# Where the operands of a matmul lie in SBUF: start addresses on multiples of 64 bytes, with a gap between held and streamed operands

## The chip, the cores and the metric

The kernel runs on one core of one Trainium2 chip. The metric is the device time of one execution in microseconds. The kernel before took 2775.96 us (median of 3 runs, 2774.65 to 2776.91). The profile is of one execution of its own.

## The reference: what is computed

One layer of an encoder over 2048 tokens of width 1024, all in float32:

```
h    = rms_norm(x) * g
proj = h @ w_in                       # 1024 -> 7 groups of 512 columns
A    = differential attention over 4 heads (block-causal mask, two softmax maps per head)
B    = HGRN2 gated linear recurrence over 4 heads, chunks of 64 tokens
x    = x + concat(A, B) @ w_out       # 1024 -> 1024
x    = x + (silu(h2 @ w_gate) * (h2 @ w_up)) @ w_down   # h2 = rms_norm(x) * g2, 1024 -> 2816 -> 1024
```

## The kernel before

All large products are made of the same piece, a matmul on TensorE of 128 rows by 128 columns held in the array against 512 columns streamed through it, in the type float32r. To keep float32 accuracy, each operand is split into a high part (a copy rounded to float32r, by ScalarE) and a low part (the remainder, by VectorE), and each product is a triple of matmuls: high by high, high by low, low by high. In a statement `pe.matmul(dst, held, streamed, ...)` the second argument is the held operand (128 columns, 512 bytes in a partition) and the third is the streamed one (512 columns, 2048 bytes in a partition). In the rows of the profile the order is the other way round: `out<-streamed,held`.

Each matmul is preceded by a weight load (LDWEIGHTS, the row PEld), which reads the held operand of the next matmul while the present one is streaming. So at nearly all times TensorE reads SBUF in two places: the streamed operand of one matmul and the held operand of another.

The kernel has four stages, one after the other:

- `project` (names `proj_`): h @ w_in in 4 blocks of 512 tokens. h of a block is in `h_hi[b % 2]` and `h_lo[b % 2]`. `h_hi[0]` is no tensor of its own: it is the tensor `lend_lent`, lent from outside. `h_hi[1]` is `proj_h_hi1`. Blocks 0 and 2 use `lend_lent`, blocks 1 and 3 use `proj_h_hi1`; nothing else differs between them. The weights are in `proj_w_hi`, `proj_w_lo`. For five of the seven groups of columns the weights are streamed and h is held (L667 to L669), for two it is the reverse (L663 to L665).
- `mix_tokens` (`att_`, `rec_`): attention and recurrence, with many small matmuls (128 or 64 columns) and some of 512 columns (`att_ring`, L1221 and L1224: keys streamed, queries held).
- `feed` (`feed_`): x + mix @ w_out, and the gate and up products, by Strassen's scheme of seven products. The held operands are `feed_a_hi`, `feed_a_lo`, the streamed ones `feed_b_hi` and `feed_b_lo`, seven of each; of the seven low parts two lie in `lend_lent` (L1867 to L1869). These go to the banks x and y, for half of the matmuls of L1868 each that the bank receives.
- `down` (`down_`): the last product, in the same scheme. Held: `down_f_hi`, `down_f_lo`; streamed: `down_w_hi`, `down_w_lo` (L2142 to L2144).

The order of the work is written out by hand in one block per engine, with semaphores between them; no scheduler or pool decides anything. Only the helper `Alloc.sb` (L75) says where a tensor lies: it takes the next free place in SBUF, so addresses follow from the order of the calls and from the sizes. A tensor starts on a multiple of 32 bytes; so a tensor of 4 bytes in a partition takes 32, and all that comes after it is displaced by 32.

Of the kernel before, what the change touches and what calls it, by code (L numbers as in the profile page):

```python
# [8 lines left out]

# [1 line left out]

# [3 lines left out]
P = 128  # L17
# [32 lines left out]
F32 = mybir.dt.float32  # L50
# [18 lines left out]
class Alloc:  # L69
# [3 lines left out]
        self.nc, self.ctx, self.prefix = nc, ctx, prefix  # L73

    def sb(self, name, shape, dt=F32):  # L75
        return self.ctx.enter_context(self.nc.sbuf_tensor(f"{self.prefix}_{name}", shape, dt))

    def bank(self, name):
        return self.ctx.enter_context(self.nc.psum_tensor(f"{self.prefix}_{name}", [P, 512], F32))
# [107 lines left out]
def project(nc, x, attn_g, w_in, q_g, k_g, ident, pair_sel, eps, out, masks, early, lambdas, subln_g, hgrn_g, w_out,  # L187
# [19 lines left out]
    with ExitStack() as ctx:  # L207
        a = Alloc(nc, ctx, "proj")
# [8 lines left out]
        warm = a.sb("warm", [P, 1])  # L217
        h_hi = [early.lent[:].rearrange("p a (s n) -> p (a s) n", n=TB), a.sb("h_hi1", [P, KS, TB], F32R)]
        h_lo = [a.sb(f"h_lo{b}", [P, KS, TB], F32R) for b in range(2)]
        w_raw = [a.sb(f"w_raw{b}", [P, KH, W]) for b in range(2)]  # L220
        w_hi = [a.sb(f"w_hi{b}", [P, KH, W], F32R) for b in range(2)]
        w_lo = [a.sb(f"w_lo{b}", [P, KH, W], F32R) for b in range(2)]
# [1119 lines left out]
def feed(nc, x, mix, ffn_g, w_gate, w_up, ident, eps, x_mid, out_operands, operands, ff, first_full, first_full_in,  # L1342
# [19 lines left out]
    with ExitStack() as ctx:  # L1362
        a = Alloc(nc, ctx, "feed")
        g_col = a.sb("g_col", [P, KS])
        full = [first_full, a.sb("full", [P, OPERANDS + 1, HALF_SLABS, P])[:]]
        a_hi = a.sb("a_hi", [P, OPERANDS, HALF_SLABS, P], F32R)
        a_lo = a.sb("a_lo", [P, OPERANDS, HALF_SLABS, P], F32R)
        b_hi = [a.sb(f"b_hi{i}", [P, HALF_SLABS * TB], F32R) for i in range(OPERANDS)]
        b_lo = [*first_b, *(a.sb(f"b_lo{i}", [P, HALF_SLABS * TB], F32R)[:] for i in range(len(first_b), OPERANDS))]
        results = [a.sb(f"results{k}", [P, 4, TB]) for k in range(2)]  # L1370
# [505 lines left out]
def down(nc, ff, w_down, x_mid, y, stored):  # L1876
# [19 lines left out]
    with ExitStack() as ctx:  # L1896
        a = Alloc(nc, ctx, "down")
        w_raw = [a.sb(f"w_raw{b}", [P, 2, D]) for b in range(RAWS)]
        w_hi = [a.sb(f"w_hi{b}", [P, SLABS, COLS], F32R) for b in range(2)]
        w_lo = [a.sb(f"w_lo{b}", [P, SLABS, COLS], F32R) for b in range(2)]  # L1900
        f_raw = [a.sb(f"f_raw{b}", [P, SLABS, P]) for b in range(2)]
        f_hi = [a.sb(f"f_hi{b}", [P, SLABS, P], F32R) for b in range(2)]
        f_lo = [a.sb(f"f_lo{b}", [P, SLABS, P], F32R) for b in range(2)]
# [244 lines left out]
def hybrid_trunk_kernel(nc, x, attn_norm_g, w_in, q_norm_g, k_norm_g, lambda_q1, lambda_k1, lambda_q2, lambda_k2,  # L2148
# [16 lines left out]
    with ExitStack() as ctx:  # L2165
        a = Alloc(nc, ctx, "all")
        ident, ones = (a.sb(n, [P, P]) for n in ("ident", "ones"))
        pair_sel = a.sb("pair_sel", [P, 2])
        eps = a.sb("eps", [P, 1])
        y_stored = [a.sem(f"y_stored{b}") for b in range(4)]  # L2170
        early_in = [a.sem(f"early_{n}_in") for n in ("k", "q", "rf", "rqk", "small")]
        first_full_in, *first_b_in = (a.sem(f"first_{n}_in") for n in ("full", "b0", "b1"))
        make_constants(nc, ident, pair_sel, ones, eps)
        with ExitStack() as whole:
            lending = Alloc(nc, whole, "lend")
            shared = lending.sb("shared", [P, 2, HEADS * TB])
            lent = lending.sb("lent", [P, 2, HALF_SLABS * TB], F32R)
            first_full = shared[:].rearrange("p a (b s n) -> p (a b) s n", s=HALF_SLABS, n=P)
            first_b = [lent[:, i, :] for i in range(2)]
            with ExitStack() as both:  # L2180
                early = First(Alloc(nc, both, "early"), early_in, shared, lent)
                masks = Alloc(nc, both, "level").sb("masks", [P, HGRN_LEVELS, HEADS // 2 * TB // 2], mybir.dt.uint8)
                last_spent = project(nc, x[0], attn_norm_g[0], w_in[0], q_norm_g[0], k_norm_g[0], ident, pair_sel, eps, mid, masks,
                                     early, (lambda_q1[0], lambda_k1[0], lambda_q2[0], lambda_k2[0]), subln_g[0], hgrn_norm_g[0],
                                     w_out[0], out_operands)

                nc.gpsimd.sem_clear(range(first_b_in[-1].num + 1, last_spent + 1))
                mix_tokens(nc, mid, ident, eps, masks, mix, early, out_operands, first_full, first_full_in, first_b, first_b_in)
            feed(nc, x[0], mix, ffn_norm_g[0], w_gate[0], w_up[0], ident, eps, x_mid, out_operands, operands, ff, first_full,
                 first_full_in, first_b, first_b_in)  # L2190
        down(nc, ff, w_down[0], x_mid, out[0], y_stored)
# [27 lines left out]
```

## Time and profile before

| | us |
|---|---|
| median of 3 runs | 2775.96 |
| the profiled execution, whole | 2776.23 |
| its span, first to last instruction | 2774.5 |
| TensorE (PE) busy | 2634.8 (95%) |
| weight loads (PEld) busy | 2214.1 (80%) |
| VectorE (DVE) busy | 1557.5 (56%) |
| ScalarE (ACT) busy | 1131.1 (41%) |
| GpSimd (POOL) busy | 896.2 (32%) |
| mean granted TensorE clock | 0.982 of full speed |

How to read it: matmuls overlap each other in the profile, since each is drawn with its way through the array (0.39 us for 512 columns), while the next one starts 0.23 us after it. So the busy time tells that TensorE always has work, but not how fast it goes. The rate is read from the distance between the starts of successive matmuls in the rows in order of time. A busy 95% together with a start every 0.23 us means that the time of the kernel is the number of matmuls by that distance, and a few waits.

The 512-column matmuls of `proj_`, `feed_` and `down_` make up some 2033 us of the 2774.5: 8904 of them at 0.2267 to 0.2332 us each.

### The profile page before, as it was taken

The page shows a single profiled execution, that of the slowest core. Times are in us where ns is not written, and L with a number is a line of the kernel's source. Part 1 is how long each engine was busy: PE and PEld are TensorE (multiplying, and loading weights), DVE is VectorE, ACT ScalarE, POOL GpSimd, SP SyncE. Part 2 cuts the span into 40 slices and gives each one's busy share as a digit, 9 for nine tenths or more (in the row PEclk, how much of TensorE's full clock was granted, in tenths as well). Part 3 has the DMA queues.
Part 4 walks back from the last instruction along what each step waited for, and adds up shares of the span by engine and source line. Part 5 has one row for each costly group of instructions (what it writes and reads, how often), then busy time and mean ns, then how long its engine had stood idle before and what let it go on. Part 6 is the DMA issues. An engine that isn't in the chain of part 4 may idle for free. (4 is left out here: it accounts for less than half of the span.)

```text
span 2774.5 us, 34306 instructions
## 1 busy us (share of the span) xinstructions
PE 2634.8 (95%) x13288; PEld 2214.1 (80%) x13288; DVE 1557.5 (56%) x1906; ACT 1131.1 (41%) x1922; POOL 896.2 (32%) x607
## 2 busy tenths in 40 slices
PE   7999999999999999986998999998999997999999
PEld 6888888887888888875776888886888885888887
DVE  5434344333676767656677565657666664356653
ACT  4434344332567666674444222224222222332231
POOL 5001100002424242303556454555454451135400
PEclk9999999999999999997998999999999998999999
DMA  4755555384343433315675334345333333777763
GB/s 154 257 181 198 172 192 198 121 282 130 100 112 102 112 101 84 92 35 197 227 254 187 98 101 111 99 114 178 110 103 104 95 102 119 260 274 266 250 208 127
DMA packets 343874, 430.48 MB, mean 155 GB/s; under 512 B 19232, under 2 KB 212768, under 8 KB 341024
## 3 DMA queue, kind: packets, MB, share of 16 engines
q1 hardware_dynamic: 343712, 428.29, 49.2%
q8 instruction: 106, 1.74, 0.3%
q14 instruction: 56, 0.46, 0.1%
HBM read 301.87 MB, written 129.50 MB: 155 GB/s over the span
## 5 line engine op out<-in xcount | busy, mean ns | idle before, releaser
L522 DVE TENSOR_TENSOR proj_w_lo<-proj_w_raw,proj_w_hi 128x2048 fp32r<-128x2048 f32 x56 | 129.8, 2318 | 233.6 <-ACT proj_w_hi L422 233.6
L2142 PE MATMUL down_prod<-down_w_hi,down_f_hi 128*128 128x512 f32 x616 | 241.2, 391 | 19.8 <-DVE down_f_lo L2078 18.9
L669 PE MATMUL proj_prod<-proj_w_hi,proj_h_lo 128*128 128x512 f32 x640 | 251.5, 393 | 0.0
L2143 PE MATMUL down_prod<-down_w_lo,down_f_hi 128*128 128x512 f32 x616 | 240.3, 390 | 0.0
L2144 PE MATMUL down_prod<-down_w_hi,down_f_lo 128*128 128x512 f32 x616 | 240.1, 390 | 0.0
L1621 ACT ACTIVATE feed_a_hi<-lend_shared 128x1024 fp32r<-128x1024 f32 (+1 forms) x78 | 94.1, 1207 | 325.7 <-PE feed_v_bank L1869 162.5
L1015 ACT ACTIVATE att_expo<-att_ring,att_neg_max 128x1024 f32<-128x1024 f32 (+4 forms) x192 | 164.8, 862 | 92.7 <-DVE att_neg_max L1126 74.0
L2048 ACT ACTIVATE down_f_hi<-down_f_raw 128x768 fp32r<-128x768 f32 x112 | 83.0, 786 | 281.8 <-PE down_prod L2144 279.0
L1621 ACT ACTIVATE feed_a_hi<-feed_full 128x1024 fp32r<-128x1024 f32 (+1 forms) x78 | 94.0, 1205 | 236.8 <-PE feed_y_bank L1869 155.2
L1867 PE MATMUL feed_y_bank<-feed_b_hi,feed_a_hi 128*128 128x512 f32 x416 | 165.7, 398 | 17.8 <-DVE feed_results L1748 17.8
L1867 PE MATMUL feed_x_bank<-feed_b_hi,feed_a_hi 128*128 128x512 f32 x416 | 163.2, 392 | 12.7 <-DVE lend_lent L1717 12.7
L1712 DVE TENSOR_TENSOR feed_a_lo<-lend_shared,feed_a_hi 128x1024 fp32r<-128x1024 f32 (+1 forms) x78 | 131.2, 1682 | 66.1 <-ACT feed_a_hi L1621 66.0
L1867 PE MATMUL feed_v_bank<-feed_b_hi,feed_a_hi 128*128 128x512 f32 x416 | 163.5, 393 | 3.4 <-DVE feed_results L1766 3.4
L1712 DVE TENSOR_TENSOR feed_a_lo<-feed_full,feed_a_hi 128x1024 fp32r<-128x1024 f32 (+1 forms) x78 | 143.3, 1837 | 40.1 <-ACT feed_a_hi L1621 40.1
L1869 PE MATMUL feed_y_bank<-feed_b_hi,feed_a_lo 128*128 128x512 f32 x416 | 164.9, 396 | 0.0
L1869 PE MATMUL feed_x_bank<-feed_b_hi,feed_a_lo 128*128 128x512 f32 x416 | 163.9, 394 | 0.0
L1868 PE MATMUL feed_v_bank<-feed_b_lo,feed_a_hi 128*128 128x512 f32 x416 | 162.6, 391 | 0.0
L1869 PE MATMUL feed_v_bank<-feed_b_hi,feed_a_lo 128*128 128x512 f32 x416 | 162.4, 390 | 0.0
L1121 DVE TENSOR_REDUCE att_run_neg_max<-att_ring 128x1 f32<-128x1024 f32 (+7 forms) x128 | 120.7, 985 | 60.6 <-PE att_ring L1224 60.6
L2142 PEld LDWEIGHTS down_prod<-down_w_hi,down_f_hi 128*128 128x128 f32 x616 | 116.0, 188 | 46.6 <-DVE down_f_lo L2078 19.8
L422 ACT ACTIVATE proj_w_hi<-proj_w_raw 128x2048 fp32r<-128x2048 f32 x56 | 107.2, 1914 | 105.8 <-PE proj_prod L669 75.2
L669 PEld LDWEIGHTS proj_prod<-proj_w_hi,proj_h_lo 128*128 128x128 f32 x640 | 120.5, 188 | 28.1
(254 smaller groups left out, 6860.4 us busy)
## 6 DMA issues: line engine op xcount, KB each, us to landing
proj_w_raw<-in_w_in_dram SPq DMA_DIRECT2D x56, 1024.0 KB, 6.5
lend_shared<-in_w_gate_dram SPq DMA_DIRECT2D x88, 256.0 KB, 4.1
feed_full<-in_w_up_dram SPq DMA_DIRECT2D x88, 256.0 KB, 4.1
ff<-feed_results SPq DMA_DIRECT2D x88, 256.0 KB, 2.6
down_w_raw<-in_w_down_dram SPq DMA_DIRECT2D x22, 1024.0 KB, 7.9
down_f_raw<-ff SPq DMA_DIRECT2D x56, 384.0 KB, 3.3
down_f_raw<-ff SPq DMA_DIRECT2D x56, 320.0 KB, 3.6
ff<-feed_ff_sum SPq DMA_DIRECT2D x66, 256.0 KB, 3.2
```

The source lines that it names most:

```text
L522: nc.vector.tensor_tensor(w_lo[n % 2][:], w_raw[n % 2][:], w_hi[n % 2][:].bitcast(F32), ALU.subtract).then_inc(w_lo_made, 1)
L669: last = pe.matmul(prod[t][:], lo[:, s, tile], wh[:, k, :], start=False, stop=stop)
L1015: nc.scalar.activation(expo[b][:, m, key:key + width], ring[:, bank * 512:bank * 512 + width], ACT.Exp, bias=neg_max[:, b, m:m + 1], accum ...
L1121: last = nc.vector.tensor_reduce(dst, ring[:, bank * 512:bank * 512 + width], AX.X, ALU.max, negate=True)
L1621: nc.scalar.activation(a_hi[:, first:end], full[g % 2][:, first:end], ACT.Copy).then_inc(a_hi_made, 1)
L1712: nc.vector.tensor_tensor(a_lo[:, first:end], full[g % 2][:, first:end], a_hi[:, first:end].bitcast(F32), ALU.subtract).then_inc(a_lo_made, 1)
L1867: pe.matmul(dst, a_hi[:, pos, s, :], hi, start=opens and s == 0, stop=False, skip_group_check=True)
L1868: pe.matmul(dst, a_hi[:, pos, s, :], lo, start=False, stop=False, skip_group_check=True)
L1869: last = pe.matmul(dst, a_lo[:, pos, s, :], hi, start=False, stop=s == HALF_SLABS - 1, skip_group_check=True)
L2142: pe.matmul(dst, hi[:, s, :], wh[:, s, :], start=opens and s == 0, stop=False, skip_group_check=True)
L2143: pe.matmul(dst, hi[:, s, :], wl[:, s, :], start=False, stop=False, skip_group_check=True)
L2144: last = pe.matmul(dst, lo[:, s, :], wh[:, s, :], start=False, stop=closes and s == SLABS - 1, skip_group_check=True)
```

## The change

The change touches addresses alone. No instruction is added, removed or reordered; the number of rows of the program is the same on each engine, and only line numbers differ (by 1 to 13).

- `Alloc.sb` rounds each tensor up to a multiple of 64 bytes: if its size in units of 32 bytes is odd, it is followed by an unused tensor of 32 bytes.
- In `project`, 128 unused bytes stand between `h_lo` and the weights; in `feed`, 128 between `a_lo` and `b_hi`; in `down`, 64 between `w_lo` and `f_raw`.

```diff
     def sb(self, name, shape, dt=F32):
-        return self.ctx.enter_context(self.nc.sbuf_tensor(f"{self.prefix}_{name}", shape, dt))
+
+        tensor = self.ctx.enter_context(self.nc.sbuf_tensor(f"{self.prefix}_{name}", shape, dt))
+        size = math.prod(shape[1:]) * (1 if dt == mybir.dt.uint8 else 4)
+        if -(-size // 32) % 2:
+            self.gap(name, 32)
+        return tensor
+
+    def gap(self, name, size):
+
+        self.ctx.enter_context(self.nc.sbuf_tensor(f"{self.prefix}_{name}_gap", [P, size // 4], F32))
...
         h_lo = [a.sb(f"h_lo{b}", [P, KS, TB], F32R) for b in range(2)]
+        a.gap("h_lo", 128)
         w_raw = [a.sb(f"w_raw{b}", [P, KH, W]) for b in range(2)]
...
         a_lo = a.sb("a_lo", [P, OPERANDS, HALF_SLABS, P], F32R)
+        a.gap("a_lo", 128)
         b_hi = [a.sb(f"b_hi{i}", [P, HALF_SLABS * TB], F32R) for i in range(OPERANDS)]
...
         w_lo = [a.sb(f"w_lo{b}", [P, SLABS, COLS], F32R) for b in range(2)]
+        a.gap("w_lo", 64)
         f_raw = [a.sb(f"f_raw{b}", [P, SLABS, P]) for b in range(2)]
```

What it does to the places that TensorE reads. Every held piece and every streamed piece begins a multiple of 512 bytes after the start of its tensor, so what two operands have to do with each other is told by their start addresses modulo 512 (bytes within a partition, from the compiled programs):

| operand | before | after |
|---|---|---|
| `lend_lent` | 192 | 256 |
| `proj_h_hi1`, `proj_h_lo` | 480 | 320 |
| `proj_w_hi`, `proj_w_lo` | 480 | 448 |
| `att_k_rest`, `att_q` (own tensors) | 256 | 384 |
| `early_k` | 192 | 256 |
| `feed_a_hi`, `feed_a_lo` | 224 | 320 |
| `feed_b_hi`, `feed_b_lo` (own tensors) | 224 | 448 |
| `down_w_hi`, `down_w_lo` | 192 | 256 |
| `down_f_hi`, `down_f_lo` | 192 | 320 |

Held less streamed, modulo 512:

| pair | before | after |
|---|---|---|
| project, h own, weights streamed | 0 | 384 |
| project, h in `lend_lent`, weights streamed | 224 | 320 |
| project, h own streamed, weights held | 0 | 128 |
| project, `lend_lent` streamed, weights held | 288 | 192 |
| feed, own tensors | 0 | 384 |
| feed, `lend_lent` streamed, a held | 32 | 64 |
| down | 0 | 64 |

Before, the distance of every pair with `lend_lent` is an odd multiple of 32, and of every other pair of the three large stages it is 0. After, every distance is a multiple of 64 and none is 0.

## Rows read from the trace of the kernel before

**Rows 1.** The page: its span, and TensorE in part 1.
```profile
span 2774.5 us, 34306 instructions
PE 2634.8 (95%) x13288; PEld 2214.1 (80%) x13288; DVE 1557.5 (56%) x1906; ACT 1131.1 (41%) x1922; POOL 896.2 (32%) x607
```

**Rows 2.** Groups of instructions by line, project: busy us, mean ns | idle before.
```profile
L667 PE MATMUL proj_prod<-proj_w_hi,lend_lent 128*128 128x512 f32 x320 | 129.9, 406 | 6.8 <-DVE proj_w_lo L522 6.0 <-DVE proj_h_lo L536 0.7
L668 PE MATMUL proj_prod<-proj_w_lo,lend_lent 128*128 128x512 f32 x320 | 127.7, 399 | 0.0
L667 PE MATMUL proj_prod<-proj_w_hi,proj_h_hi 128*128 128x512 f32 x320 | 125.7, 393 | 0.0
L668 PE MATMUL proj_prod<-proj_w_lo,proj_h_hi 128*128 128x512 f32 x320 | 124.6, 389 | 0.0
...
L663 PE MATMUL proj_prod<-lend_lent,proj_w_hi 128*128 128x512 f32 x128 | 51.1, 399 | 0.0
L663 PE MATMUL proj_prod<-proj_h_hi,proj_w_hi 128*128 128x512 f32 x128 | 50.2, 392 | 0.0
```

**Rows 3.** The same view, feed and down.
```profile
L2142 PE MATMUL down_prod<-down_w_hi,down_f_hi 128*128 128x512 f32 x616 | 241.2, 391 | 19.8 <-DVE down_f_lo L2078 18.9 <-DVE down_w_lo L2072 0.8
...
L1867 PE MATMUL feed_y_bank<-feed_b_hi,feed_a_hi 128*128 128x512 f32 x416 | 165.7, 398 | 17.8 <-DVE feed_results L1748 17.8
...
L1867 PE MATMUL feed_v_bank<-feed_b_hi,feed_a_hi 128*128 128x512 f32 x416 | 163.5, 393 | 3.4 <-DVE feed_results L1766 3.4
L1867 PE MATMUL feed_x_bank<-feed_b_hi,feed_a_hi 128*128 128x512 f32 x416 | 163.2, 392 | 12.7 <-DVE lend_lent L1717 12.7
...
L1868 PE MATMUL feed_x_bank<-lend_lent,feed_a_hi 128*128 128x512 f32 x208 | 83.5, 401 | 0.0
...
L1868 PE MATMUL feed_y_bank<-lend_lent,feed_a_hi 128*128 128x512 f32 x208 | 82.6, 397 | 0.0
L1867 PE MATMUL feed_z_bank<-feed_b_hi,feed_a_hi 128*128 128x512 f32 x208 | 81.0, 390 | 0.4 <-DVE feed_b_lo L1717 0.4
...
L1868 PE MATMUL feed_x_bank<-feed_b_lo,feed_a_hi 128*128 128x512 f32 x208 | 80.9, 389 | 0.0
```

**Rows 4.** TensorE in time, project, block 0: start us, us, what; 89 rows, ends.
```profile
99.38 0.39 PE L664 MATMUL proj_prod<-proj_h_lo,proj_w_hi 128*128 128x512 f32 x1
...
119.90 0.39 PE L669 MATMUL proj_prod<-proj_w_hi,proj_h_lo 128*128 128x512 f32 x1
```

**Rows 5.** The same, block 1 (`proj_h_hi1`): 112 rows, ends.
```profile
249.78 0.39 PE L664 MATMUL proj_prod<-proj_h_lo,proj_w_hi 128*128 128x512 f32 x1
...
274.94 0.39 PE L664 MATMUL proj_prod<-proj_h_lo,proj_w_hi 128*128 128x512 f32 x1
```

**Rows 6.** The same, feed with `lend_lent`: 15 rows, ends.
```profile
2139.45 0.40 PE L1869 MATMUL feed_x_bank<-feed_b_hi,feed_a_lo 128*128 128x512 f32 x1
...
2142.68 0.40 PE L1868 MATMUL feed_y_bank<-lend_lent,feed_a_hi 128*128 128x512 f32 x1
```

**Rows 7.** The same, down: 134 rows, ends.
```profile
2449.71 0.39 PE L2143 MATMUL down_prod<-down_w_lo,down_f_hi 128*128 128x512 f32 x1
...
2479.85 0.39 PE L2144 MATMUL down_prod<-down_w_hi,down_f_lo 128*128 128x512 f32 x1
```

**Rows 8.** The same, feed, first matmuls of 512 columns after transposes.
```profile
1308.22 0.40 PE L1868 MATMUL feed_y_bank<-feed_b_lo,feed_a_hi 128*128 128x512 f32 x1
...
1308.69 0.39 PE L1867 MATMUL feed_y_bank<-feed_b_hi,feed_a_hi 128*128 128x512 f32 x1
1308.91 0.39 PE L1868 MATMUL feed_y_bank<-feed_b_lo,feed_a_hi 128*128 128x512 f32 x1
...
1309.84 0.39 PE L1869 MATMUL feed_y_bank<-feed_b_hi,feed_a_lo 128*128 128x512 f32 x1
```

**Rows 9.** Who waited for whom: us in total, times, longest.
```profile
ACT down_f_hi L2048 <- PE down_prod L2144: 279.0, 53, 6.0
ACT feed_a_hi L1621 <- PE feed_y_bank L1869: 272.9, 80, 11.5
...
DVE proj_w_lo L522 <- ACT proj_w_hi L422: 233.6, 56, 12.4
```

More of the change, by code:

```diff
@@ L12 @@
+import math
 from contextlib import ExitStack
```

## The prediction

> **What bounds the kernel now.** I read first the span and busy times of the page: TensorE is busy for 2634.8 of 2774.5 us, no other engine for more than 56% [rows 1]. Then the groups by line: the triples of 512-column matmuls of project, feed and down carry the time, and the idle time ahead of them is small, 6.8 us at the most in project, 17.8 and 12.7 in feed, 19.8 in down [rows 2, 3]. Then the waits: the longest ones are of ScalarE for TensorE, 279.0 us in down and 272.9 in feed; VectorE waits 233.6 us for ScalarE in project, with TensorE going on [rows 9]. So TensorE is the bound in these stages, and a matmul that costs less there shortens the kernel.
>
> The view that decides is the last, TensorE's rows in order of time, since the distance between starts is what a matmul costs. In a stretch of project with h in `lend_lent`, 89 rows in a row without a gap go from 99.38 to 119.90 us: 20.52 / 88 = 0.2332 us each [rows 4]. In a stretch of the block with `proj_h_hi1`, 112 rows take 25.16 us: / 111 = 0.2267 [rows 5]. In feed, where one of three streamed operands is `lend_lent`, 15 rows take 3.23 us: / 14 = 0.2307, which is one hundredth of a microsecond in 3.23 uncertain [rows 6]. In down, 134 rows take 30.14 us: / 133 = 0.2266 [rows 7]. At the 2.4 GHz that the granted clock of 1.0 in these stretches stands for, streaming 512 columns takes 213.3 ns, so even the best stretch has 13 ns a matmul too much.
>
> The same instructions on the same weights, in blocks that differ only in where h lies, are 6.5 ns apart. The groups by line say it too: L667 has a mean of 406 ns with `lend_lent` and 393 without, L668 399 and 389, L663 399 and 392; in feed L1868 has 401 with `lend_lent` and 389 without [rows 2, 3]. Since TensorE reads the next held operand while it streams, I take it that the two reads get into each other's way, and that their distance modulo some small power of two sets how much: 0 costs 13 ns, an odd multiple of 32 costs 20.
>
> One more thing is in the rows. After transposes, the first 512-column matmuls of feed with distance 0 are not at 0.2267: from 1308.22 to 1309.84 us seven steps take 1.62, that is 0.2314, and the steps vary, one of them being 0.22 [rows 8]. Only later do they settle. So the cost depends on how the two reads meet in time as well, and 0.2267 is a state into which the sequence falls, not a constant of the address.
>
> **The change, part by part.** It is addresses only, so the sum is a count of matmuls by a difference of steps.
>
> *Multiples of 64.* All distances that were odd multiples of 32 are now even ones. In project with `lend_lent` there are 320 triples with h held and 128 with h streamed [rows 2]: 448 x 3 = 1344 matmuls. If they go from 0.2332 to 0.2267, that is 1344 x 6.5 ns = 8.7 us. In feed `lend_lent` is in 208 + 208 = 416 triples [rows 3], 1248 matmuls, which go from 0.2307 to 0.2267: 5.0 us. Together 13.7 us. The two ends: 0, if what matters is a coarser distance than 64 (then 64 is as bad as 32), and 13.7 us. What speaks for the upper end is that the stages at distance 0 hold 0.2267 with held pieces at any multiple of 512. I take 13.7.
>
> *Gaps of 128 and 64.* All 8904 matmuls (448 + 448 triples in project; 1456 in feed, from 416 + 416 + 416 + 208 of L1867; 616 in down; 2968 x 3) [rows 2, 3] now have a distance that is not 0. The trace has no long stretch at such a distance, so this is the unknown term. One end: the reads no longer meet, and a step is 213.3 ns; the other: the settled state of distance 0 is lost, and each step costs the unsettled mean, 231.4 ns [rows 8]. Against 226.7, these are -13.4 and +4.7 ns a matmul, -119 us over all 8904 and, for the 6312 without `lend_lent` alone, +30 us. The nearest row to a better state is the shortest step of rows 8, 1308.69 to 1308.91, shown as 0.22; as its neighbours average 0.231 I read it as 0.224 (an estimate from the rounded starts; it could be up to 0.225 and some less). It shows that one meeting of the reads at 2.7 ns less is possible; that a whole sequence holds it isn't shown. I take half of that way, 1.3 ns: 8904 x 1.3 = 11.6 us.
>
> *Everything else.* The attention stage has some 500 matmuls of 512 columns, in groups of 2 to 7 that never settle; at 5 ns either way this is under 3 us, put at 0. The 32-byte shifts of the operands of ScalarE, VectorE, GpSimd and of the DMAs are put at nothing: these engines wait for TensorE by the hundreds of microseconds [rows 9], and a few per cent of their operations stay under that cover. Should TensorE become so fast that the cover goes, the first to be late is VectorE in feed, the one whose results it waits for even now (17.8 us) [rows 3].
>
> Sum for the profiled execution, 2776.2 us whole (span 2774.5 and 1.7 around it; the median of the runs is 2776.0, so nothing has to be shifted): 2776.2 - 13.7 - 11.6 = 2750.9, say 2750.
>
> **The rule that speaks against it.** The rows show 0.2332 beside 0.2267 us for the same lines with another place of h [rows 4, 5]. The Trainium skill, "TensorE: Matmul & The Clock Gate", section "Step-by-step: what each phase is for", says that TensorE has two independent SBUF read ports and that loading the next weights takes nothing from the running matmul; "SBUF — State Buffer", section "Who interferes with whom", says that TensorE never waits for anyone there. By that rule no address would matter and the time would stay at 2776. By this trace it doesn't hold in full.
>
> **The rivals.**
>
> *Alignment helps, the gaps do nothing.* A sequence at any constant distance that is a multiple of 64 settles into the same state, since the two reads shift in time against each other until they fit. For it: the settling in rows 8, and that down and own-tensor project have the same 0.2267 [rows 5, 7]. Time: 2776.2 - 13.7 = 2762.5.
>
> *No change at all.* Either what slows the `lend_lent` blocks isn't the 32 bytes but the mixture of distances in a triple (in project 224, 224, 0), which goes on after the change (320, 320, 384), and a constant distance costs the same everywhere; or reads do not interfere and the difference has another source in that tensor. For it: in the mixed triples the matmul with own-tensor operands, L669 or L1869, is slow as well, as the even 0.2332 over all rows shows [rows 4]. Time: 2776.
>
> *Slower: the settled state is lost.* At a distance of 0 modulo 512 the sequence holds 0.2267. If this state exists only there, the change takes it away in down (64), feed (384) and project (384, 128), and all 6312 matmuls outside `lend_lent` go at 0.2314: 6312 x 4.7 ns = 30 us; `lend_lent` stays where it is. Time: 2806. It decides even against a full gain of the alignment if more than about 2900 matmuls (13.7 us / 4.7 ns) lose the state; feed with own tensors, 3120 of them, is enough. For it: it is the only state seen to hold in 25 to 30 us without a break [rows 5, 7]; against it: that an unsettled sequence at all distances would have to find no state of its own.
>
> *Conflicts gone.* 213.3 ns a step: 8904 steps make 1899 us in place of 1344 x 0.2332 + 1248 x 0.2307 + 6312 x 0.2267 = 2032. Time: 2776 - 133 = 2643. Against it: no step in the rows is under 0.22.
>
> **How the numbers follow.** The forecast (both help, the gaps by a little) 0.42, its own range 2735 to 2762; alignment alone 0.20 (2762.5); no change 0.12 (2776); slower 0.18 (2806, or less where only one stage loses its state); conflicts gone 0.08 (2643). Faster by over 0.2% (5.5 us, about what a measurement of this kernel can tell from no change) is 0.42 + 0.20 + 0.08 = 0.70, the same 0.12, slower 0.18. The range of 8 in 10 takes in the forecast, alignment alone, no change, and the third of the slower case in which one stage alone loses its state: 2700 to 2795. Below, it reaches to gaps that are worth some 7 ns a matmul.
>
> **What would show it.** In the changed kernel, TensorE's rows in time: project with `lend_lent` at 0.2267 or under (alignment right), at 0.233 (wrong); down at 0.224 to 0.226 (gap right), at 0.2267 (gaps do nothing), at 0.231 and never settling (slower rival), at 0.215 (conflicts gone). Down has no `lend_lent` and was at distance 0, so it tells the gap alone; project before and after tells both. The groups by line should show L667 with `lend_lent` and with `proj_h_hi` at the same mean. ScalarE's waits for TensorE should shrink by what TensorE gains. The prediction is wrong if the gain is in the attention stage or in waits rather than in the steps, or if down moves opposite to project.

## The result and the profile after

The changed kernel takes 2809.2 us (median of 4 runs, 2808.45 to 2811.59) beside 2776.4 us of the kernel before on the same chips: 1.0119 times, 95% interval 1.0106 to 1.0133. It is slower by some 33 us; 2750 was forecast, with 2700 to 2795 as the range.

The page, in the rows that answer to [rows 1], shows the same instructions, with TensorE busy 36 us longer:

```profile
span 2807.6 us, 34306 instructions
...
PE 2671.0 (95%) x13288; PEld 2220.0 (79%) x13288; DVE 1550.5 (55%) x1906; ACT 1129.8 (40%) x1922; POOL 896.2 (32%) x607
```

By stage (TensorE alone; columns: stretch in us from the span's start, its length, PE busy with the count of matmuls, granted clock, share of the DMA engines, GB/s), first the kernel before, cut at the ends of project, mix_tokens and feed:

```profile
0.00:669.00 669.00, 650.99 (x2942) 1.00 0.56 188
669.00:1262.00 593.00, 536.82 (x4004) 0.97 0.37 100
1262.00:2340.00 1078.00, 1024.66 (x4496) 0.98 0.44 135
2340.00:2775.00 435.00, 422.29 (x1848) 0.99 0.70 232
```

and the changed one:

```profile
0.00:675.00 675.00, 656.93 (x2944) 1.00 0.55 186
675.00:1268.00 593.00, 537.48 (x4000) 0.96 0.36 100
1268.00:2361.00 1093.00, 1042.02 (x4496) 0.98 0.43 133
2361.00:2808.00 447.00, 434.59 (x1848) 0.98 0.68 226
```

Project is 6 us longer, feed 15, down 12, the attention stage as before. TensorE's busy time grows by 5.9, 17.4 and 12.3 us; in feed some of it goes into waits that it had anyway. The granted clock is the same (0.981 over the span, 0.982 before), so it isn't the clock.

TensorE's rows in order of time (start us, us, what), first down, which answers to [rows 7], 131 rows without a gap:

```profile
2479.65 0.39 PE L2156 MATMUL down_prod<-down_w_lo,down_f_hi 128*128 128x512 f32 x1
...
2509.99 0.39 PE L2157 MATMUL down_prod<-down_w_hi,down_f_lo 128*128 128x512 f32 x1
```

30.34 / 130 = 0.2334 us a matmul, where it was 0.2266. Project with `proj_h_hi1`, which answers to [rows 5], 109 rows:

```profile
249.64 0.39 PE L675 MATMUL proj_prod<-proj_h_lo,proj_w_hi 128*128 128x512 f32 x1
...
274.84 0.39 PE L675 MATMUL proj_prod<-proj_h_lo,proj_w_hi 128*128 128x512 f32 x1
```

25.20 / 108 = 0.2333 for 0.2267. Project with `lend_lent`, which answers to [rows 4], 88 rows:

```profile
99.79 0.40 PE L674 MATMUL proj_prod<-lend_lent,proj_w_hi 128*128 128x512 f32 x1
...
119.99 0.40 PE L678 MATMUL proj_prod<-proj_w_hi,lend_lent 128*128 128x512 f32 x1
```

20.20 / 87 = 0.2322 for 0.2332: here the change gains a little. The groups by line, which answer to [rows 2, 3] (busy us, mean ns | idle before), say the same, and also that the waits ahead of the largest groups are about what they were (19.5 us for 19.8 in down, 17.7 for 17.8 in feed):

```profile
L2155 PE MATMUL down_prod<-down_w_hi,down_f_hi 128*128 128x512 f32 x616 | 245.1, 398 | 19.5 <-DVE down_f_lo L2091 19.3 <-DVE down_w_lo L2085 0.2
...
L1879 PE MATMUL feed_y_bank<-feed_b_hi,feed_a_hi 128*128 128x512 f32 x416 | 166.3, 400 | 17.7 <-DVE feed_results L1760 17.7
...
L678 PE MATMUL proj_prod<-proj_w_hi,proj_h_hi 128*128 128x512 f32 x320 | 127.3, 398 | 0.0
...
L679 PE MATMUL proj_prod<-proj_w_lo,proj_h_hi 128*128 128x512 f32 x320 | 126.3, 395 | 0.0
L679 PE MATMUL proj_prod<-proj_w_lo,lend_lent 128*128 128x512 f32 x320 | 125.8, 393 | 0.0
...
L1880 PE MATMUL feed_x_bank<-lend_lent,feed_a_hi 128*128 128x512 f32 x208 | 83.1, 399 | 0.0
```

L679 (L668 before) has 395 ns with `proj_h_hi` for 389, and 393 with `lend_lent` for 399: the two have changed places. ScalarE's waits for TensorE, which answer to [rows 9], grow with TensorE's steps:

```profile
ACT feed_a_hi L1633 <- PE feed_y_bank L1881: 295.6, 84, 11.3
ACT down_f_hi L2061 <- PE down_prod L2157: 291.2, 53, 6.2
```

The sum of the steps nearly closes. Over all starts that are under 300 ns apart in both traces, the mean step changes like this:

| matmuls of 512 columns | number | before, ns | after, ns | together, us |
|---|---|---|---|---|
| down | 1848 | 226.7 | 233.3 | +12.1 |
| feed without `lend_lent` | 3120 | 226.9 | 232.4 | +16.9 |
| feed with `lend_lent` | 1248 | 231.1 | 231.6 | +0.6 |
| project, own h held | 960 | 227.2 | 232.8 | +5.3 |
| project, own h streamed | 384 | 227.0 | 233.1 | +2.3 |
| project, `lend_lent` held | 960 | 233.1 | 231.2 | -1.8 |
| project, `lend_lent` streamed | 384 | 233.0 | 232.0 | -0.4 |

Together that is 35 us, beside 36.2 more of busy time and 33.1 more of span; TensorE's idle time is 3.1 us less (136.6 for 139.7).

### The profile page after: what moved, and what is told of

Same layout as the page of the kernel before. It is cut to its first block and busy times, and to the rows that moved or that the text cites. A ratio compares the mean times of both kernels' runs of the same rounds, so it can differ in the third digit from the quotient of the medians.

```text
span 2807.6 us, 34306 instructions
## 1 busy us (share of the span) xinstructions
PE 2671.0 (95%) x13288; PEld 2220.0 (79%) x13288; DVE 1550.5 (55%) x1906; ACT 1129.8 (40%) x1922; POOL 896.2 (32%) x607
## 5 line engine op out<-in xcount | busy, mean ns | idle before, releaser
L2155 PE MATMUL down_prod<-down_w_hi,down_f_hi 128*128 128x512 f32 x616 | 245.1, 398 | 19.5 <-DVE down_f_lo L2091 19.3
L1879 PE MATMUL feed_y_bank<-feed_b_hi,feed_a_hi 128*128 128x512 f32 x416 | 166.3, 400 | 17.7 <-DVE feed_results L1760 17.7
L1724 DVE TENSOR_TENSOR feed_a_lo<-feed_full,feed_a_hi 128x1024 fp32r<-128x1024 f32 (+1 forms) x78 | 139.7, 1791 | 40.2 <-ACT feed_a_hi L1633 40.2
```

The source lines that it names most:

```text
L1724: nc.vector.tensor_tensor(a_lo[:, first:end], full[g % 2][:, first:end], a_hi[:, first:end].bitcast(F32), ALU.subtract).then_inc(a_lo_made, 1)
L1879: pe.matmul(dst, a_hi[:, pos, s, :], hi, start=opens and s == 0, stop=False, skip_group_check=True)
L2155: pe.matmul(dst, hi[:, s, :], wh[:, s, :], start=opens and s == 0, stop=False, skip_group_check=True)
```

## The experiments

Ahead of the runs stood the theory that the slower rival had put: at a distance of 0 (held less streamed, by start addresses) the sequence of matmuls settles at 226.7 ns, and the gaps took that away. "Distance" is modulo 512 bytes below, until the runs reduce it. The two operands that meet are the one being streamed and the one being loaded beside it for the next matmul.

**The rounding alone.** The changed kernel without its gaps:

```diff
         h_lo = [a.sb(f"h_lo{b}", [P, KS, TB], F32R) for b in range(2)]
-        a.gap("h_lo", 128)
...
-        a.gap("a_lo", 128)
...
-        a.gap("w_lo", 64)
```

> The rounding to 64 bytes alone, without the three gaps. Own-tensor operands are at distance 0 modulo 512 again, lend_lent 64 from the rest. Theory 1 (the gaps took the settled state of distance 0 away): down and the triples without lend_lent are back at 226.7 ns a matmul, those with lend_lent stay at 231 to 233; time 2770 to 2778 us. Rival (the rounding, by what it does to absolute addresses, is what slows): down stays at 233 ns, time 2800 to 2812 us. Second rival (64 bytes from the rest is as good as 0 for a triple with lend_lent): those at 226.7 too, time about 2762 us.

Measured: 2772.3 us, 0.9986 times the kernel before (0.9976 to 0.9995). Down is at 226.7 ns again, and so are the settled stretches of project and feed without `lend_lent`. In down 135 rows take 30.38 us, / 134 = 0.2267:

```profile
2449.62 0.39 PE L2154 MATMUL down_prod<-down_w_hi,down_f_lo 128*128 128x512 f32 x1
...
2480.00 0.39 PE L2153 MATMUL down_prod<-down_w_lo,down_f_hi 128*128 128x512 f32 x1
```

The triples with `lend_lent`, 64 bytes from the rest, have 229.2 ns in project with h held and 229.4 in feed, less than at odd multiples of 32 (233.1 and 231.1), but not 226.7. In project with h streamed they have 234.0, where they had 233.0: this got worse, and it is outside the 231 to 233 that were expected. So the first theory holds for the operands that are back at distance 0, and the rounding is worth some 4 us by itself, where 13.7 was forecast.

**The gaps alone**, the other half: the kernel before with the three gaps and no rounding.

```diff
         h_lo = [a.sb(f"h_lo{b}", [P, KS, TB], F32R) for b in range(2)]
+        a.gap("h_lo", 128)
...
         a_lo = a.sb("a_lo", [P, OPERANDS, HALF_SLABS, P], F32R)
+        a.gap("a_lo", 128)
...
         w_lo = [a.sb(f"w_lo{b}", [P, SLABS, COLS], F32R) for b in range(2)]
+        a.gap("w_lo", 64)
```

> The three gaps alone, without the rounding to 64 bytes. Distances of own-tensor operands are 64 (down), 384 (feed) and 384, 128 (project), as in the changed kernel; those with lend_lent are odd multiples of 32. Theory (what the change costs is the loss of the settled state at distance 0, and the rounding only moves lend_lent by a little): down at 233.3, own-tensor triples of feed and project at 232 to 233, lend_lent at 231 to 234; time 2776 + 6312 x 6 ns = 2814 us, less 2 for the beginnings, 2808 to 2816 us. Rival (the two parts cost only together): 2776 to 2790 us.

Measured: 2808.2 us, 1.0116 times (1.0099 to 1.0132), as the whole change. In down 130 rows take 30.11 us, / 129 = 0.2334:

```profile
2479.78 0.40 PE L2150 MATMUL down_prod<-down_w_hi,down_f_hi 128*128 128x512 f32 x1
...
2509.89 0.39 PE L2150 MATMUL down_prod<-down_w_hi,down_f_hi 128*128 128x512 f32 x1
```

The gaps carry the whole loss. The two parts do not add up: the 4 us of the rounding are not there when the gaps are (2808.2 us without it, 2809.2 with it).

**Everything at distance 0.** The kernel before, with two pieces of padding that bring h, the weights and feed's operands to the residue of `lend_lent`, 192:

```diff
+        a.gap("h_hi", 224)
         h_hi = [early.lent[:].rearrange("p a (s n) -> p (a s) n", n=TB), a.sb("h_hi1", [P, KS, TB], F32R)]
...
         g_col = a.sb("g_col", [P, KS])
+        a.gap("g_col", 480)
         full = [first_full, a.sb("full", [P, OPERANDS + 1, HALF_SLABS, P])[:]]
```

> The kernel before with 224 unused bytes ahead of proj_h_hi1 and 480 behind feed's g_col, so that every held and streamed operand of project and feed, lend_lent among them, is at distance 0 modulo 512. Theory 1 (distance 0 is what lets the steps settle at 226.7 ns): all triples of project and feed at 226.7, time 2776.4 - 1344 x 6.5 ns - 1248 x 4.4 ns = 2762 us. Rival (lend_lent is slow for another reason than its distance): its triples stay at 233 and 231 ns, time 2776 us.

Measured: 2764.0 us, 0.9952 times (0.9940 to 0.9965), 12 us less than before by the medians (2775.9) and 13 by the ratio. The theory's number was 2762. All settled steps are at 226.7 ns, those with `lend_lent` too, and the groups show it: L673, L674 and L1875 here are L667, L668 and L1868 of [rows 2, 3].

```profile
L673 PE MATMUL proj_prod<-proj_w_hi,lend_lent 128*128 128x512 f32 x320 | 127.8, 399 | 6.8 <-DVE proj_w_lo L528 6.0 <-DVE proj_h_lo L542 0.8
L673 PE MATMUL proj_prod<-proj_w_hi,proj_h_hi 128*128 128x512 f32 x320 | 125.6, 393 | 0.0
L674 PE MATMUL proj_prod<-proj_w_lo,lend_lent 128*128 128x512 f32 x320 | 125.4, 392 | 0.0
...
L1875 PE MATMUL feed_x_bank<-lend_lent,feed_a_hi 128*128 128x512 f32 x208 | 81.9, 394 | 0.0
L1875 PE MATMUL feed_y_bank<-lend_lent,feed_a_hi 128*128 128x512 f32 x208 | 80.9, 389 | 0.0
```

About half of what is left between 399 and 393 ns in L673 is in the first twelve matmuls of block 0, from 20.9 to 25.7 us, four of which are of L673: the granted clock is 0.50 there, TensorE's lower level of 1.2 GHz, after a stretch in which it was nearly idle (3.7 us busy of 20), and most of the twelve have 0.63 us in place of 0.39. In the starts, which the comparison rests on, nothing is left: the steps from the tenth on behind a break have 226.7 ns in both blocks. So `lend_lent` was slow for its distance.

**The attention stage as well.** The same with `a.gap("first", 448)` ahead of att's tensors.

> As e2_zero, and 448 unused bytes ahead of att's tensors, so that keys and queries of the attention stage, too, are at distance 0 from one another and from lend_lent. Theory: its some 500 matmuls of 512 columns stand in groups of 2 to 7, too short to settle, so the gain over e2_zero is 0 to 2 us: 2761 to 2764 us. Rival (a mixture of distances costs 6 ns a matmul there too): 500 x 6 ns = 3 us, and the groups of att_ring have a mean that is 6 ns less.

Measured: 2764.5 us, 0.9955 times (0.9942 to 0.9967), no different from the run before it. Where two 512-column matmuls of `att_ring` follow each other within 250 ns (185 times), the mean step is 231.5 ns here and 231.3 without that padding: they come in groups of one to seven, shorter than the nine steps that settling takes elsewhere (below).

**Which distances settle.** Two sweeps give each of the two buffers of an operand a place of its own, so that one run holds four distances in down and four more in project. In down, where w0, w1 are the streamed and f0, f1 the held buffers, the first sweep has this (the second puts 256 bytes more ahead of f0):

```diff
-        w_hi = [a.sb(f"w_hi{b}", [P, SLABS, COLS], F32R) for b in range(2)]
-        w_lo = [a.sb(f"w_lo{b}", [P, SLABS, COLS], F32R) for b in range(2)]
+        w_hi, w_lo = [], []
+        for k, part in enumerate((w_hi, w_lo)):
+            part.append(a.sb(f"w_part{k}0", [P, SLABS, COLS], F32R))
+            a.gap(f"w_up{k}", 448)
+            part.append(a.sb(f"w_part{k}1", [P, SLABS, COLS], F32R))
+            a.gap(f"w_down{k}", 64)
...
+        for k, part in enumerate((f_hi, f_lo)):
+            part.append(a.sb(f"f_part{k}0", [P, SLABS, P], F32R))
+            a.gap(f"f_up{k}", 128)
...
```

> Distances (held less streamed, modulo 512) by buffer: in down 0, 64 for f_hi0 and 128, 192 for f_hi1, by w_hi0 and w_hi1; in project 32, 160 (blocks 0 and 2) and 224, 352 (blocks 1 and 3), with the negatives where h is streamed; feed all 0. Theory 1: 226.7 ns in down's 0 and in feed, 230 to 234 at every other distance. Rival (each distance has a settled state of its own level): levels that differ, some perhaps under 226.7. Second rival (only whether a distance is constant counts, so that distance 64 costs the same as 0 in long stretches): all of down at one level.

> As the sweep before it, with 256, 320 (f_hi0) and 384, 448 (f_hi1) in down, and 96, 128 and 352, 384 in project. Theory 1 in its form with a period of 512 bytes: none at 226.7, all at 230 to 234 ns. If the period is 256 bytes: the distance 256 is at 226.7. If it is 128: 256 and 384 are.

Measured (2785.2 and 2789.0 us, single runs): one stretch of down in the first sweep passes from distance 0 to 128 at 2604.54 us, when `f_hi1` is held in place of `f_hi0`, the streamed buffer being the same:

```profile
2599.78 0.39 PE L2170 MATMUL down_prod<-down_w_part,down_f_part 128*128 128x512 f32 x1
...
2604.54 0.40 PE L2170 MATMUL down_prod<-down_w_part,down_f_part 128*128 128x512 f32 x1
...
2611.99 0.39 PE L2169 MATMUL down_prod<-down_w_part,down_f_part 128*128 128x512 f32 x1
```

21 steps of 0.2267 us (4.76 us) and then 32 of 0.2328 (7.45 us). The means by distance, worked out from all starts of the two traces, from the tenth step in a row at one distance on:

| held less streamed, modulo 512 | mean step, ns | where |
|---|---|---|
| 0 | 226.7 | down, feed |
| 256 | 226.7 | down |
| 32 | 233.5 | project |
| 64, 320 | 233.3, 233.3 | down |
| 96 | 234.0 | project |
| 128, 384 | 232.3, 232.4 | down |
| 128, 384 | 232.6, 232.7 | project |
| 160, 416 | 233.3, 233.3 | project |
| 192, 448 | 231.1, 231.1 | down |
| 224, 480 | 233.3, 233.4 | project |
| 352 | 234.3 | project |

Two distances that are 256 apart have the same value within 0.3 ns: the period is 256 bytes, so my modulus of 512 was twice too large, and of the multiples of 32 only 0 has the low level. The best of the others is 192. The 64 and 128 of the changed kernel are among the others. Away from 0 the distance isn't all: at 128, with h streamed, the same lines of project have 233.3 ns in the changed kernel and 232.5 with the gaps alone, and what differs there is only where the whole lies.

**The same gaps at 256.** If so, the changed kernel needs no more than another number:

```diff
-        a.gap("h_lo", 128)
+        a.gap("h_lo", 256)
...
-        a.gap("a_lo", 128)
+        a.gap("a_lo", 256)
...
-        a.gap("w_lo", 64)
+        a.gap("w_lo", 256)
```

> The changed kernel with its three gaps at 256 bytes in place of 128, 128 and 64, nothing else. Theory (the settled state at 226.7 ns comes back every 256 bytes of distance, and the gaps of 128 and 64 took it away): down, and the triples of project and feed without lend_lent, at 226.7 ns; those with lend_lent, 64 from the rest, at 229 to 231 as with the rounding alone; time 2768 to 2775 us. Rival (any gap, or what it displaces behind it, slows): 2795 to 2812 us, down at 231 to 234 ns.

Measured: 2773.2 us, 0.9985 times (0.9976 to 0.9995), as with the rounding alone. In down 134 rows take 30.15 us, / 133 = 0.2267:

```profile
2449.74 0.39 PE L2155 MATMUL down_prod<-down_w_hi,down_f_hi 128*128 128x512 f32 x1
...
2479.89 0.39 PE L2156 MATMUL down_prod<-down_w_lo,down_f_hi 128*128 128x512 f32 x1
```

The settled steps of feed (226.8) and of project (226.7) at distance 256 say the same. The triples with `lend_lent` are again at 229.1 and 229.4, and at 234.0 with h streamed, over the 231 that was expected. A gap does no harm by itself; its size modulo 256 does.

**Small distances.** In down each tensor is 256 bytes longer and its operand begins a few bytes further in:

```diff
+        w_hi, w_lo = ([a.sb(f"w_{part}{b}", [P, SLABS * COLS + 64], F32R)[:, at // 4:at // 4 + SLABS * COLS]
+                       .rearrange("p (s n) -> p s n", n=COLS) for b, at in enumerate((32, 40))] for part in ("hi", "lo"))
...
+        f_hi, f_lo = ([a.sb(f"f_{part}{b}", [P, SLABS * P + 64], F32R)[:, at // 4:at // 4 + SLABS * P]
+                       .rearrange("p (s n) -> p s n", n=P) for b, at in enumerate((48, 16))] for part in ("hi", "lo"))
```

> As e2_zero, with small distances in down: held less streamed 16 and -16 by f_hi0 and f_hi1 with w_hi0, and 8 and -24 with w_hi1 (modulo 256). Theory A (the reads meet by pieces of 32 or 64 bytes, so that less than that changes nothing): 226.7 ns at 8 and 16. Theory B (each few bytes shift the two reads in time against each other, and only multiples of 256 are equal): 230 to 234 ns at all four. A third way: somewhere near 0 a step below 226.7 ns, which would be the better place for the operands.

> As e8_fine, with held less streamed 4 and -4 bytes (f_hi0, f_hi1 with w_hi0) and -8 and -16 (with w_hi1). If only a distance of 0 modulo 256 settles at 226.7 ns: all at 228 to 234. If the reads go by pieces of 16 bytes, as -16 at 228.0 beside 16 at 232.4 would allow: 4 at 226.7 and the negative ones at 228. If small distances don't matter: 226.7 at 4 and -4.

(In this second one `at` is 32, 44 for w and 36, 28 for f.) Measured (2770.3 and 2773.7 us, single runs), mean settled steps in ns: 4 bytes 232.3, 8 bytes 231.9, 16 bytes 232.3; -4 bytes 233.1, -8 bytes 231.1, -16 bytes 228.0 in the one and 228.9 in the other, -24 bytes 234.8. Four bytes are enough to lose the state, against the theory of pieces of 32 or 64 bytes; nothing near 0 is under 226.7; and -16, with two values, shows again that away from 0 the distance alone doesn't say it all.

**What the extra 13 ns are.** I had taken them to be collisions of the stream with the load of the next held operand. Then a shorter load must cost less. In the first kernel two of three matmuls of a triple in down hold 64 columns, in the others nearly all hold 64 or 32:

```diff
-                    pe.matmul(dst, hi[:, s, :], wl[:, s, :], start=False, stop=False, skip_group_check=True)
+                    pe.matmul(dst[0:64], hi[:, s, 0:64], wl[:, s, :], start=False, stop=False, skip_group_check=True)
```

> As e2_zero, but in down the second and third matmul of each triple hold only 64 columns in place of 128, into the first 64 rows of the product; this leaves out the low parts for the other 64 rows. The streams are the same. Theory (the 13.4 ns over 213.3 that a settled step costs are collisions with the load of the next held operand, so many for each byte of the load): two of three loads are half as long, so the mean step in down falls by 2/3 x 6.7 = 4.4 ns to about 222 ns. Rival (the extra is the stream's own, say a fixed loss for each 64 bytes, whatever is loaded beside it): down stays at 226.7 ns.

> As e2_zero, but in down every matmul except the one that opens a sum holds 64 columns in place of 128; this leaves out the last 64 rows of each product. In e7_half_load the mixture of 128 and 64 may have broken the settled state; here nearly all loads are alike. If the extra over 213.3 ns is collisions in proportion to the bytes loaded: 13.4 / 2 = 6.7 ns, down at 220 ns. If it is the stream's own, or set by the place of the start alone: 226 to 231 ns as before.

> The same with 32 columns held. In proportion to the bytes loaded: 213.3 + 3.4 = 217 ns in down. Independent of them: 226 to 231 ns.

Measured (2770.4, 2771.1, 2775.5 us, single runs): down has mean steps of 229.5, 230.0 and 231.7 ns. Less to load made it slower than the 226.7 ns of e2_zero, in all three, and both values expected of the first of them (222 and 226.7) were missed. That the loads are indeed shorter shows in their own rows (PEld; mean ns behind the busy time), of e2_zero

```profile
L2151 PEld LDWEIGHTS down_prod<-down_w_hi,down_f_lo 128*128 128x128 f32 x616 | 116.1, 188 | 24.1
```

of the kernel with 64 columns held throughout

```profile
L2152 PEld LDWEIGHTS down_prod<-down_w_hi,down_f_lo 128*64 128x64 f32 x616 | 83.1, 135 | 59.5 <-issue 1.0
```

and of the one with 32

```profile
L2152 PEld LDWEIGHTS down_prod<-down_w_hi,down_f_lo 128*32 128x32 f32 x616 | 67.3, 109 | 76.0 <-issue 0.8
```

So a cost in proportion to the bytes loaded is refuted: 220 and 217 ns were expected by it with 64 and 32 columns. What the runs do show is that the held operand's place matters (the streamed one unchanged at 2604.54 us above), and that its length matters too. Why a shorter load costs more isn't shown. With 64 columns the steps run through 224 to 236 ns over and over, as they do ahead of the settled stretch in [rows 8], so it looks as if the low state were undone; this is a reading and was not tested.

## Why the prediction was wrong

- *What bounds the kernel.* Right. The stages that were named as bound by TensorE's steps are those that moved, by 6, 15 and 12 us, and the sum of the steps, 35 us, gives the difference of the spans, 33.1, within 2 us.
- *Multiples of 64, put at 13.7 us.* The direction was right, the size wrong. Measured alone it is 4 us (0.9986), and in the whole change 1.6 us (the rows of `lend_lent` in the table above). The step that failed is "if they go from 0.2332 to 0.2267": alone they went to 229.2 and 229.4 ns with h held and in feed, and to 234.0 with h streamed, since a distance of 64 has no settled state at 226.7 either (233.3 in down). The end of "64 is as bad as 32" was named and not taken. What 13.7 us priced is distance 0 for all, and there it was right: 12 to 13 us.
- *The gaps, put at 11.6 us of gain.* This is the step that made the prediction wrong. I took half the way to 0.224 from one short step of an unsettled sequence [rows 8], in place of asking what the distance does to the settled one. The gaps cost 1.0116 alone, 32 us. Per matmul the whole change costs 6.6 ns in down, 5.5 in feed, 5.6 and 6.1 in project, where the bound on the bad side had been 4.7: the mean of an unsettled sequence isn't the worst, since a sequence at distance 64 repeats 236 and 231 ns for as long as it lasts, a mean of 233.3.
- *The rival that came true* is the third, "the settled state is lost": 2806 for 2809. Its condition (the state exists only at distance 0) holds with the period of 256 bytes in place of 512. I gave it 0.18, for the reason that a sequence at any constant distance would shift in time until it fits. The sweeps refute this: at the other multiples of 32 it stays at 231.1 to 234.3 ns, however long it lasts. That 2806 is so near is in part luck: the rival's 4.7 ns a matmul was too small (30 us where these matmuls lost 37), and the gain of `lend_lent` and the shorter waits, which it left out, made up for it.
- *Everything else at 0.* Right: the attention stage moved by less than 1 us, and padding its operands to distance 0 brought nothing either.
- *The rule that speaks against it.* The Trainium skill, "TensorE: Matmul & The Clock Gate", section "Step-by-step: what each phase is for", has the load of the next weights take nothing from the running matmul. These runs show a step of 0.2328 us in place of 0.2267 from the moment at which only the held operand lies elsewhere (2604.54 us in the first sweep), and the same instructions of down at 233.3 for 226.7 ns with other addresses; the measurement decides.
- *The cause, as far as it goes.* Shown: the step depends on the distance of held and streamed operand with a period of 256 bytes, and 0 is the only one of 15 distances tried, counted modulo 256, at which it is 226.7. Not shown: by what the two reads meet, why 0 leaves 13 ns over 213.3, and why a shorter load makes the step longer. Whether absolute addresses matter was not varied by itself. Distance 0 gave 226.7 at the residues 192, 224, 256, 320 and 480, so there they do not; at distance 128 something beside the distance is worth 0.8 ns (233.3 and 232.5), and what it is stays open.

## What to carry to other kernels

Where a float32r kernel is bound by long rows of matmuls (128 columns held, 512 streamed, another held operand each, the form measured here), lay all held and all streamed operands at the same address modulo 256 bytes in a partition, lent tensors included. Padding of 704 bytes in two places brought 0.5% here; the wrong padding costs 1.2%. Read it off as the distance between starts, and read it where the sequence has settled: the busy share of TensorE is 95% in all cases.

## What the runs showed of the hardware that had not been expected

- The step of a 512-column float32r matmul has levels by the distance of held and streamed operand, 226.7 ns at multiples of 256 bytes, 231.1 to 234.3 at the other multiples of 32, and 228.0 to 234.8 at the distances under 32 that were tried.
- It is a state of the sequence: at distance 0 it is reached some nine steps after a break, with a mean of 229.5 ns on the way in project and 230.4 in feed (e2_zero), and of 231.4 in the short stretch of [rows 8].
- A held operand of 64 or 32 columns makes the step longer, not shorter (230.0 and 231.7 for 226.7 ns), though the load itself falls from 188 to 135 and 109 ns.
